# Setup of a hybrid encoder step: pieces of the modulation matrix as the stationary operand, in full precision, instead of split halves as the moving operand

## The reference, cut to what matters

```
mod = silu(c) @ w_ada + b_ada                  # w_ada: 1024 x 6144, float32
sh1, sc1, g1, sh2, sc2, g2 = split(mod, 6)
hn = rmsnorm(x, ln1_g) * (1 + sc1) + sh1       # needed by everything after
... four mixers on hn, then  x = x + g1 * mix
h2 = rmsnorm(x, ln2_g) * (1 + sc2) + sh2
x = x + g2 * (relu(h2 @ mlp_w1)**2 @ mlp_w2)
```

## Time and profile before

| | us |
|---|---|
| median of 3 runs | 3482.82 (3482.36 to 3483.55) |
| profiled execution, span | 3482.2 |
| TensorE matmul busy | 3062.8 (88%) |
| VectorE busy | 1662.6 (48%) |
| ScalarE busy | 1316.4 (38%) |
| GpSimd busy | 910.7 (26%) |

### The profile page before, as it was taken

One profiled execution on the slowest core, in us unless ns is written; L12 is line 12 of the kernel. 1 busy time (PEld: TensorE's weight loads), 2 busy tenths in 40 slices (PEclk: granted clock), 3 DMA queues, 4 the chain that ended last, 5 costly groups with the idle time before them and its releaser, 6 DMA issues. The chain is left out here.

```text
span 3482.2 us, 43476 instructions
## 1 busy us (share of the span) xinstructions
PE 3062.8 (88%) x15985; PEld 2660.8 (76%) x15985; DVE 1662.6 (48%) x2420; ACT 1316.4 (38%) x1876; POOL 910.7 (26%) x472
## 2 busy tenths in 40 slices
PE   4797899688977889767897699999999999999997
PEld 1475676466755667545686599999999999999997
DVE  4417215641367413677302444455655456655555
ACT  3436335543455434455312422223532225432222
POOL 0231233023300233000200433334633326522330
PEclk9899899788977889777855799999999999999998
DMA  7231323022300223000241422222232121222210
GB/s 260 87 111 41 97 61 97 1 70 64 103 18 0 69 64 103 18 0 0 88 125 43 148 73 67 66 72 61 73 128 72 60 72 54 81 94 72 72 60 34
DMA packets 305776, 251.06 MB, mean 72 GB/s; under 512 B 10747, under 2 KB 268134, under 8 KB 305638
## 3 DMA queue, kind: packets, MB, share of 16 engines
q1 hardware_dynamic: 287238, 219.30, 21.0%
q10 hardware_dynamic: 18400, 29.89, 2.4%
HBM read 223.13 MB, written 21.70 MB: 70 GB/s over the span
## 5 line engine op out<-in xcount | busy, mean ns | idle before, releaser
L1658 DVE SCALAR_TENSOR_TENSOR xs<-op,modT,xs 128x352 f32<-128x352 f32 (+1 forms) x896 | 454.7, 528 | 201.5 <-PE op L1753 199.9
L1732 PE MATMUL hp<-h_hi,w1h 128*128 128x352 f32 x1536 | 497.5, 324 | 13.6 <-POOL h_lo L1482 13.6
L1751 PE MATMUL op<-g_hi,w2h 128*128 128x352 f32 x1536 | 501.0, 326 | 1.5 <-DVE xs L1658 1.1
L1733 PE MATMUL hp<-h_lo,w1h 128*128 128x352 f32 x1536 | 496.8, 323 | 0.0
L1734 PE MATMUL hp<-h_hi,w1l 128*128 128x352 f32 x1536 | 496.0, 323 | 0.0
L1752 PE MATMUL op<-g_lo,w2h 128*128 128x352 f32 x1536 | 495.1, 322 | 0.0
L1753 PE MATMUL op<-g_hi,w2l 128*128 128x352 f32 x1536 | 494.5, 322 | 0.0
L610 POOL TENSOR_TENSOR w_lo<-wraw,w_hi 128x1024 fp32r<-128x1024 f32 x122 | 297.1, 2436 | 461.6 <-ACT w_hi L646 452.5
L1471 POOL TENSOR_TENSOR w1l<-w1r,w1h 128x1024 fp32r<-128x1024 f32 x96 | 230.5, 2402 | 616.5 <-ACT w1h L1513 616.5
L1116 PE MATMUL zp<-hn_hi,w_hi 128*128 128x512 f32 x960 | 383.5, 399 | 2.4 <-POOL w_lo L610 1.8
L1120 PE MATMUL zp<-hn_lo,w_hi 128*128 128x512 f32 x960 | 376.4, 392 | 2.5 <-POOL hn_lo L627 2.5
(11 more groups left out here) (256 smaller groups left out, 4531.8 us busy)
## 6 DMA issues: line engine op xcount, KB each, us to landing
wraw<-in_w_in_dram SPq DMA_DIRECT2D x96, 512.0 KB, 3.8
w1r<-in_mlp_w_dram SPq DMA_DIRECT2D x96, 512.0 KB, 4.1
w2r<-in_mlp_w_dram SPq DMA_DIRECT2D x96, 512.0 KB, 3.3
wraw<-in_w_out_dram SPq DMA_DIRECT2D x34, 512.0 KB, 4.0
wada<-in_w_ada_dram ACTq DMA_DIRECT2D x6, 2048.0 KB, 9.7
wada<-in_w_ada_dram SPq DMA_DIRECT2D x6, 2048.0 KB, 8.7
xs<-x_scratch SPq DMA_DIRECT2D x3, 2816.0 KB, 12.2
oT<-in_x_prompt_dram SPq DMA_DIRECT2D x4, 2048.0 KB, 7.9
```

Of the source, the lines that this page charges most:

```text
L1658: ins = dve.scalar_tensor_tensor(out=cols, in0=op[i % 4][:, a:e], scalar=modT[:, M_G2 + d, m:m + 1], in1=cols, op0=ALU.mult, op1=ALU.add)
L1732: pe.matmul(bank, w1h[ft][:, k, :], h_hi[:, k, cols], start=(k == 0), stop=False)
L1733: pe.matmul(bank, w1h[ft][:, k, :], h_lo[:, k, cols], start=False, stop=False)
L1751: pe.matmul(bank, wh, g_hi[odd][:, ft, cols], start=(ft == 0), stop=False)
```

## The change

The split goes. The piece itself, in float32, is the stationary operand, 128 x 128 at a time; the two conditions `csil` are two moving columns. The product lands in `pm` directly as columns, 128 output features on the partitions, so the row copy and the transpositions go as well. ScalarE no longer works on the pieces; it only issues its loads. A piece's buffer is loaded again when TensorE has used it (`wada_used`). VectorE waits for the last piece and does its additions without the low part's.

```diff
-        wada_hi = [sb(f"wada_hi{i}", [P, KT, CH], F32R) for i in range(2)]
-        wada_lo = [sb(f"wada_lo{i}", [P, KT, CH], F32R) for i in range(2)]
-        chl = sb("chl", [P, KT, 4], F32R)
-        mod_rows = sb("mod_rows", [4, 6 * D_MODEL])
...
-        pr = ctx.enter_context(nc.psum_tensor("pr", [4, 2, CH], F32))
-        pm = ctx.enter_context(nc.psum_tensor("pm", [P, 48, 4], F32))
+        pm = ctx.enter_context(nc.psum_tensor("pm", [P, 48, 2], F32))
...
         def load_wada(eng, c):
-            wait(eng, wada_lo_ok, c - RING + 1)
+            wait(eng, wada_used, c - RING + 1)
...
         # ScalarE
-            act.wait_ge(silu_c, 1)
-            act.activation(chl[:, :, 0:2], csil[...], ACT.Copy).then_inc(c_hi, 1)
...
-            for c in range(NCH):
-                act.wait_ge(wada_in[c % RING], 16 * (c // RING + 1))
-                wait(act, row_full, c - 1)
-                act.activation(wada_hi[c % 2][:, :, :], wada[c % RING][:, :, :], ACT.Copy).then_inc(wada_hi_ok, 1)
-                if c >= 1 and c % 2 == 0 and c + RING - 1 < NCH:
-                    load_wada(act, c + RING - 1)
+            for c in range(RING + 1, NCH, 2):
+                load_wada(act, c)
...
         # VectorE
-            dve.tensor_tensor(chl[:, :, 2:4], csil[...], chl[:, :, 0:2].bitcast(F32), ALU.subtract).then_inc(c_lo, 1)
-            def take_row(c): ...
-            for c in range(NCH):
-                dve.wait_ge(wada_hi_ok, c + 1)
-                dve.tensor_tensor(wada_lo[c % 2][:, :, :], wada[c % RING][:, :, :],
-                                  wada_hi[c % 2][:, :, :].bitcast(F32), ALU.subtract).then_inc(wada_lo_ok, 1)
-                if c:
-                    take_row(c - 1)
-            take_row(NCH - 1)
-            dve.wait_ge(mod_full, 1)
+            dve.wait_ge(wada_used, NCH)
             for c in range(2):
                 chain.link(dve.tensor_tensor(const["modT"][:, :, c], pm[:, :, c], ..., ALU.add))
-                chain.link(dve.tensor_tensor(const["modT"][:, :, c], const["modT"][:, :, c], pm[:, :, 2 + c], ALU.add))
...
         # TensorE
-            pe.wait_ge(c_lo, 1)
-            def turn_row(c): ...
+            pe.wait_ge(silu_c, 1)
             for c in range(NCH):
-                pe.wait_ge(wada_lo_ok, c + 1)
-                wait(pe, row_read, c - 1)
-                for k in range(KT):
-                    pe.matmul(pr[:, c % 2, :], chl[:, k, :], wada_hi[c % 2][:, k, :], start=(k == 0), stop=False)
-                    ins = pe.matmul(pr[:, c % 2, :], chl[:, k, :], wada_lo[c % 2][:, k, :], start=False,
-                                    stop=(k == KT - 1))
-                ins.then_inc(row_full, 1)
-                if c:
-                    turn_row(c - 1)
-            turn_row(NCH - 1).then_inc(mod_full, 1)
+                pe.wait_ge(wada_in[c % RING], 16 * (c // RING + 1))
+                for i in range(CT):
+                    for k in range(KT):
+                        ins = pe.matmul(pm[:, c * CT + i, :], wada[c % RING][:, k, i * P:(i + 1) * P], csil[:, :, k],
+                                        start=(k == 0), stop=(k == KT - 1))
+                ins.then_inc(wada_used, 1)
```

More of the change, by code:

```diff
@@ L174, in setup_phase @@
         pt = ctx.enter_context(nc.psum_tensor("pt", [P, 2, 512], F32))
-        pr = ctx.enter_context(nc.psum_tensor("pr", [4, 2, CH], F32))
-        pm = ctx.enter_context(nc.psum_tensor("pm", [P, 48, 4], F32))
+        pm = ctx.enter_context(nc.psum_tensor("pm", [P, 48, 2], F32))
         rows_in, wada_in = [sem("rows_in1"), sem("rows_in2")], [sem(f"wada_in{i}") for i in range(RING)]
-        wada_hi_ok, wada_lo_ok, row_full, row_read, c_hi, c_lo = (
-            sem("wada_hi_ok"), sem("wada_lo_ok"), sem("row_full"), sem("row_read"), sem("c_hi"), sem("c_lo"))
+        wada_used = sem("wada_used")
         zeroed, blocks_in, masks = sem("zeroed"), sem("blocks_in"), sem("masks")
-        rows_t, prm, silu_c, mod_full = sem("rows_t"), sem("prm"), sem("silu_c"), sem("mod_full")
+        rows_t, prm, silu_c = sem("rows_t"), sem("prm"), sem("silu_c")
         act_chain, dve_chain, lra_hi_ok, lra_in, lam_a = (
@@ L266, in _ @@
                            ACT.Silu).then_inc(silu_c, 1)
-            act.wait_ge(silu_c, 1)
-            act.activation(chl[:, :, 0:2], csil[:, :, :].rearrange("p c k -> p k c"), ACT.Copy).then_inc(c_hi, 1)
             act.wait_ge(lra_in, 16)
@@ L324, in _ @@
                                              const["prm1"][:, R1_BADA:R1_BADA + 48], ALU.add))
-                chain.link(dve.tensor_tensor(const["modT"][:, :, c], const["modT"][:, :, c], pm[:, :, 2 + c],
-                                             ALU.add))
             for gs, m, g in ((const["gs1"], M_SC1, R2_LN1), (const["gs2"], M_SC2, R2_LN2)):
@@ L339, in _ @@
             pe.transpose(pt[:, 1, 0:R2_ALL], rows2[:, :], const["ident"][0:R2_ALL, 0:R2_ALL]).then_inc(rows_t, 1)
-            pe.wait_ge(c_lo, 1)
[L342 to L347, removed]
-            for c in range(NCH):
-                pe.wait_ge(wada_lo_ok, c + 1)
-                wait(pe, row_read, c - 1)
-                for k in range(KT):
-                    pe.matmul(pr[:, c % 2, :], chl[:, k, :], wada_hi[c % 2][:, k, :], start=(k == 0), stop=False)
-                    ins = pe.matmul(pr[:, c % 2, :], chl[:, k, :], wada_lo[c % 2][:, k, :], start=False,
-                                    stop=(k == KT - 1))
-                ins.then_inc(row_full, 1)
-                if c:
-                    turn_row(c - 1)
-            turn_row(NCH - 1).then_inc(mod_full, 1)
+            pe.wait_ge(silu_c, 1)
+            for c in range(NCH):
+                pe.wait_ge(wada_in[c % RING], 16 * (c // RING + 1))
[4 more added lines that the diff above has]
+                ins.then_inc(wada_used, 1)
 def mixer_phase(nc, const, mixc, x_prompt, x_sample, state_gla, cache_sb_k, cache_sb_v, w_in, w_out,
```

## The result

The change makes the kernel slower: 3551.25 us (median of 4 runs, 3549.32 to 3555.6) against 3482.59 us. The ratio is 1.0198, with an interval of 1.0184 to 1.0213. The forecast was 3554 us, 2.0% slower.

A forecast was written before the change was run, and what follows sets the result against it. Setup was taken as a serial prefix, bound by a ring of hand-overs among three engines. 27.3 + 163.9 us plus a short tail put the mixer at 193.2, +71.1 us: 3554 us, 2.0% slower, range 3541 to 3568.

The forecast's parts named there:

- The start: In setup, the first new product on TensorE was put at 27.3 us, after the second row-tile transposition.
- The products: Setup's new TensorE stream: 768 records 213 ns apart, 163.9 us in all.
- The count: Setup's 384 products were to be two matmul records each, 768 records.
- The clock: TensorE was to be granted 0.50 (1.2 GHz) through some 164 us of setup's products.
- What hides: Setup's matrix loads were to hide behind TensorE's 13.7 us per piece, with some 30 us to spare.
- The tail: End of setup: VectorE's two additions and gain products, 0.48 + 0.77 us, then 0.54 us to the mixer's first transposition.
- The rest: The mixer, from about 193 us on, was to run as before; its opening could move the time some 3 us.
- The sum: Whole kernel: mixer from 193.2 us, +71.1 us, span 3553.3 us; timed median 0.6 us above the span.
- The load sets the pace: In setup's products, the 128-column weight load was to fix 213 ns a record; two moving columns save nothing against 64.
- halving the stationary columns halves the record: Read from the mixer's decode part: 110 ns a record with 64 stationary columns against 213 with 128.
- the rival of an alternating clock: Setup's products at a clock alternating as in the old stream: 127 ns a record, time 3488 us; chance 0.04.

The follow-up runs named there:

- hi_only: The new kernel with only the rounded half of each piece, in the reduced type, as stationary operand, remainder left out: 3481.66 us.
- warm: The new kernel with twelve dummy products of 512 columns on TensorE before setup's products: 3556.32 us.
- warm2: The new kernel with twenty-four dummy products of 512 columns, so TensorE is still at work when setup's products begin: 3551.07 us.
- cols64: The new kernel with the moving operand widened from 2 to 64 columns, 62 of them zeros: 3558.32 us.
- stat64: The new kernel with stationary pieces of 64 columns instead of 128, 1536 records: 3515.57 us.
- stat32: The new kernel with stationary pieces of 32 columns instead of 128, 3072 records: 3521.62 us.

## Why the prediction was right, point by point

- The start: 27.3 us forecast, 27.47 measured.
- The products: 768 records 213 ns apart, as forecast. The stream of 163.9 us took 163.6 from first to last start. The count (two records a product) is right, and `hi_only` shows the reason.
- The clock: 0.50, right, shown by `warm` and `warm2` and by the mixer's first transpositions, not by the new kernel's own clock column. The forecast had the level by precedent, from lines 1126 and 1269; line 1221, of the shape of line 1126, had run at 1.00. `warm2` shows how both can be: a stream of loads entered at 1.00 kept that for 2.3 us, and line 1221's run lasts 3.78 us. Why the level falls was not forecast and stays open.
- What hides: no wait before any record, right. The tail: VectorE ended at 192.77 us and the mixer began at 193.31, forecast 193.2.
- The rest: forecast unchanged within 3 us; it was 5.2 us shorter. This is not an effect that can be ascribed to the change: over the 14 profiled executions of the table, all with the same code after setup, the rest lies between 3354.8 and 3363.5 us, and kernels with the same setup length differ by as much (`cols64` 3362.7, `warm2` 3355.2). The bound of 3 us was too small for that spread.
- The sum: 3553.3 us of span forecast, 3548.1 measured (the 5.2 us of the rest); that run's time stands 2.0 us above its span, not 0.6, so 3550.07, and the median is 1.2 us above it. From 3554 to 3551.25 is thus two errors of opposite sign outside setup.
- The load sets the pace, and two columns save nothing against 64: right, shown by `cols64`. The step from line 1269 to "halving the stationary columns halves the record" is right too, though the averages of `stat64` (82 ns) and `stat32` (42) seem to deny it: within a group the records are 107 and 53 ns apart.
- Misread: the mean clock of 0.88, from which the rival of an alternating clock was priced. Its first 5.9 us have no clock record and ran at the low pace, so the old stream had full clock for some 0.68 of the stretch, not 0.76. The forecast's own sum does not use it.

So the change removed three engines' hand-overs (setup from 39 to 122 us) and put 164 us of TensorE in their place, because 768 loads of 128 columns at 1.2 GHz, with two columns' use of each, take longer than 192 streams of 512 columns did.

## What to carry to other kernels

When one side of a product is only a few columns wide, price both orders by what TensorE does per record: a load of 128 x 128 took 213 ns at the low clock and 112 at the high one with up to 128 columns moving past it, and full precision doubled the count. Take the pace from a row of the same stationary shape, and with it the clock that the trace shows for a stage that does nothing else. Before an average pace is called a price, look whether the distances behind it are all alike. And a narrow operand can be stationary in several groups of output rows at once, which here turned the loss into a gain of 1.1%.

## What the runs showed that was not expected

- Zeros made it faster: 128 moving columns instead of 2, with the same loads, took the mixer's start from 193.31 to 117.71 us: the records halved with the clock. Why the chip granted the one stream 2.4 GHz and the other 1.2 stays open.
- Small pieces were cheaper than their loads: 82 and 42 ns on average for 64 and 32 columns, where one load costs 107 and 53, since groups that write to different output rows overlapped by four records at each change.
- Four groups of two output rows ran side by side: 16 records of 512 columns in 1.90 us at the high clock and 3.60 at the low one.
- The clock column shows 1.00 where the trace has no clock record yet; two kernels with the same 213 ns showed 1.00 (the change) and 0.50 (`warm`).
